# Fourier stage of a two-block network: its inputs loaded in the projection before it, the attention's queries loaded after its channel step

## The reference

```python
def fourier_mix(u, w_four):
    B, L, _ = u.shape
    ug = u.astype(jnp.float32).reshape(B, L, FOUR_GROUPS, FOUR_DIM)
    f = jnp.fft.fft2(ug, axes=(1, 3), norm="ortho").real
    return f.reshape(B, L, D_FOUR).astype(u.dtype) @ w_four

(fx, fgx, nqx, nkx, nvx, ngx, gqx, gkx, gvx, ggx, zfx, zbx) = jnp.split(hx @ w_in[l], IN_SPLITS, axis=-1)
na_x = neighbourhood_attention(split_heads(nqx, NA_HEADS), split_heads(nkx, NA_HEADS),
                               split_heads(nvx, NA_HEADS), nkc_h, nvc_h, rpb[l])
four_x = fourier_mix(fx, w_four[l])
mix_x = jnp.concatenate([four_x * jax.nn.silu(fgx), na_x * jax.nn.silu(ngx), gla_x * jax.nn.silu(ggx)], axis=-1)
x_new = x + gate_x[:, None, :] * (mix_x @ w_out[l])
```

## Time and profile before

| | us |
|---|---|
| median of the 3 runs | 4332.79 |
| lowest and highest run | 4326.86, 4337.24 |
| the profiled execution, span from its first to its last instruction | 4326.4 |
| PE busy in it | 3967.8 (92%) |
| DVE, ACT, POOL busy | 2036.2, 1432.6, 683.4 |
| Fourier block, first layer: first issue to the next block's first issue | 786.0 to 883.6 |
| Fourier block, second layer: first issue, and first POOL instruction of the next block | 2155.7, 2245.8 |

### The profile page before, as it was taken

How to read it: one execution, slowest core, us unless ns; L and a number is a source line. 1 busy time by engine, 2 the same in 40 slices (tenths; PEclk the granted TensorE clock), 3 DMA queues, 4 the chain that set the end, 5 groups by cost and what they waited for, 6 DMA issues and landing times. The chain is left out here.

```text
span 4326.4 us, 66533 instructions
## 1 busy us (share of the span) xinstructions
PE 3967.8 (92%) x25359; PEld 3241.8 (75%) x25359; DVE 2036.2 (47%) x4616; ACT 1432.6 (33%) x3255; POOL 683.4 (16%) x761
## 2 busy tenths in 40 slices
PE   6999999899679799999999869799999989979799
PEld 4777789777568688778977658677777867868687
DVE  5365111167656542111127567632750456657554
ACT  5000444256422310144327523321111467721211
POOL 3021000223120210000032220131430001000100
PEclk8999999999889899999999989899999989989899
DMA  5244221731256422222273345432111143357221
GB/s 195 90 147 143 82 77 61 230 136 59 100 196 220 175 100 73 95 76 77 75 240 106 113 146 198 173 112 90 64 71 66 47 134 102 103 214 255 79 77 64
DMA packets 215264, 525.90 MB, mean 122 GB/s; under 512 B 27478, under 2 KB 88392, under 8 KB 205604
## 3 DMA queue, kind: packets, MB, share of 16 engines
q1 hardware_dynamic: 188740, 438.91, 29.2%
q0 software_dynamic: 26208, 82.74, 5.4%
HBM read 330.43 MB, written 191.13 MB: 121 GB/s over the span
## 5 line engine op out<-in xcount | busy, mean ns | idle before, releaser
L72 PE MATMUL tm_tacc<-tm_tw_hi,hT_hi 128*128 128x384 f32 (+1 forms) x1120 | 414.6, 370 | 17.2 <-DVE tm_tw_lo L906 10.0
L73 PE MATMUL tm_tacc<-tm_tw_lo,hT_hi 128*128 128x384 f32 (+1 forms) x1120 | 410.0, 366 | 0.0
L74 PE MATMUL tm_tacc<-tm_tw_hi,hT_lo 128*128 128x384 f32 (+1 forms) x1120 | 410.0, 366 | 0.0
L72 PE MATMUL tz_tacc<-tz_tw_hi,hT_hi 128*128 128x512 f32 x896 | 359.4, 401 | 6.0 <-POOL tz_tw_lo L935 4.1
L72 PE MATMUL cm_acc<-hT_hi,cm_wb_hi 128*128 128x512 f32 (+1 forms) x912 | 362.2, 397 | 0.0
L73 PE MATMUL tz_tacc<-tz_tw_lo,hT_hi 128*128 128x512 f32 x896 | 355.0, 396 | 0.0
L74 PE MATMUL tz_tacc<-tz_tw_hi,hT_lo 128*128 128x512 f32 x896 | 355.0, 396 | 0.0
L74 PE MATMUL cm_acc<-hT_hi,cm_wb_lo 128*128 128x512 f32 (+1 forms) x912 | 344.3, 378 | 0.0
L73 PE MATMUL cm_acc<-hT_lo,cm_wb_hi 128*128 128x512 f32 (+1 forms) x912 | 343.9, 377 | 0.0
L788 DVE SCALAR_TENSOR_TENSOR tm_ds<-tm_dg,tm_ds 128x512 f32<-128x512 f32 (+1 forms) x40 | 25.6, 639 | 532.1 <-ACT tm_ds L782 532.1
L72 PEld LDWEIGHTS tm_tacc<-tm_tw_hi,hT_hi 128*128 128x128 f32 x1120 | 210.9, 188 | 59.1 <-DVE tm_tw_lo L906 13.6
(11 more groups left out here) (405 smaller groups left out, 8770.1 us busy)
## 6 DMA issues: line engine op xcount, KB each, us to landing
scr_z<-tz_tz SPq DMA_DIRECT2D x112, 256.0 KB
scr_zcm<-cm_zo SPq DMA_DIRECT2D x96, 256.0 KB, 2.0
scr_ztm<-tm_tz SPq DMA_DIRECT2D x68, 256.0 KB, 2.0
scr_xres<-out_x POOLq DMA_DIRECT2D x34, 512.0 KB, 4.1
cm_area<-in_w_ada POOLq DMA_DIRECT2D x64, 256.0 KB, 3.0
scr_z<-out_xn POOLq DMA_DIRECT2D x32, 512.0 KB, 4.8
mo_z<-scr_z SPq DMA_DIRECT2D x16, 1024.0 KB
tz_traw<-in_w_in SPq DMA_DIRECT2D x7, 2048.0 KB, 8.4
```

What stands on the lines that cost most here:

```text
L72: nc.tensor.matmul(out, ah, bh, start=start, stop=False)
L73: nc.tensor.matmul(out, ah, bl, start=False, stop=False)
L74: return nc.tensor.matmul(out, al, bh, start=False, stop=stop)
```

## The change

- `project_tm` gets `ahead`, a `FourierInputs`. In the last chunk, after the store of tile 3, SP waits until the last weights have been split (from then on `traw` is free) and issues `dch`, `wf` and image channels 0 to 127, `fx[0]` (1024 KB), into the place of `traw`. After the store of the last tile but one, SP waits for `decays.finished` and issues image channels 128 to 255, `fx[1]` (1024 KB), into the place of the decay buffers. The wait for the decay sums at the block's end goes.
- `fourier_phase` no longer issues `dch`, `wf` and `fx`. The context's channels come by themselves (`fc`, 256 KB, first layer only). PE waits for `f0_in` and `f1_in` in place of `fx_in`, and for `fc_in` ahead of the context's tiles.
- The queries' space is the one in which `dch`, `wf` and `fx[0]` lie, so SP issues the keys first, then waits for the 16th tile of the channel step (`ab_mm` at `N2`), then issues the queries, and only then goes on to the stores of `yo`.
- The buffers of the Fourier phase are moved by two gaps, so that `yo` and `fc` lie in the place of `fx[1]`.

```diff
@@ project_tm, SP
                     sp.dma_start(dst(c, t), zo[n % 3][:, 0:widths[c]]).then_inc(z_out[n % 3], 16)
+                    if ahead and c == n_chunks - 1 and t == 3:
+                        sp.wait_ge(lo_dve, KC // 2 * n_chunks)
+                        sp.wait_ge(lo_pool, KC // 2 * n_chunks)
+                        ahead.first(sp)
+                    if ahead and c == n_chunks - 1 and t == tiles[c] - 2:
+                        decays.finished(sp)
+                        ahead.second(sp)
             total = at[n_chunks]
             for j in range(3):
                 sp.wait_ge(z_out[j], 16 * ((total + 2 - j) // 3))
-            if decays:
+            if decays and not ahead:
                 decays.finished(sp)
@@ FourierInputs
+    def place(self, name):
+        at = lambda n, shape, offset: self.nc.alloc_sbuf_tensor_at(f"{name}_{n}", shape, F32, offset=offset)
+        self.dch, self.wf = at("dch", [128, 2, 2, 256], self.raw_at), at("wf", [128, 2, 256], self.raw_at + 4096)
+        self.fx = [at("fx0", [128, LX], self.raw_at + 6144), at("fx1", [128, LX], self.sums_at)]
+
+    def first(self, sp):
+        l, io = self.l, self.io
+        self.place(f"fa{l}")
+        sp.dma_start(self.dch[:, :, :, :], io["dft_ch"]).then_inc(self.w_in, 16)
+        sp.dma_start(self.wf[:, :, :], io["w_four"][l:l + 1, :, :, :].rearrange("a p k n -> p (a k) n")).then_inc(self.w_in, 16)
+        sp.dma_start(self.fx[0][:, :], io["zcm"][0, :, 0:LX]).then_inc(self.f0_in, 16)
+
+    def second(self, sp):
+        sp.dma_start(self.fx[1][:, :], self.io["zcm"][1, :, 0:LX]).then_inc(self.f1_in, 16)
@@ fourier_phase, SP
-                sp.dma_start(dch[:, :, :, :], io["dft_ch"]).then_inc(w_in, 16)
-                sp.dma_start(wf[:, :, :], io["w_four"][l:l + 1, :, :, :].rearrange("a p k n -> p (a k) n")).then_inc(w_in, 16)
-                sp.dma_start(fx[:, :, 0:LF], io["zcm"][0:2, :, 0:LF].rearrange("c p t -> p c t")).then_inc(fx_in, 16)
                 sp.dma_start(d1[:, :, :, :], io["dft_1"]).then_inc(d1_in, 16)
                 sp.dma_start(d2[:, :, :], io["dft_2"]).then_inc(d2_in, 16)
                 sp.dma_start(dc[:, :, :, :], io["dft_ctx"]).then_inc(d2_in, 16)
+                if first:
+                    sp.dma_start(fc[:, :, :], io["zcm"][0:2, :, LX:LT].rearrange("c p t -> p c t")).then_inc(fc_in, 16)
                 na.load_lines(sp, io)
-                na.load_tokens(sp, io)
+                na.load_keys(sp, io)
+                sp.wait_ge(ab_mm, N2)
+                na.load_queries(sp, io)
@@ fourier_phase, PE
-                pe.wait_ge(w_in, 32)
+                pe.wait_ge(fi.w_in, 32)
...
-                pe.wait_ge(fx_in, 16)
+                pe.wait_ge(fi.f0_in, 16)
+                pe.wait_ge(fi.f1_in, 16)
```

More of the change, by code:

```diff
@@ L709, in __init__ @@
     def __init__(self, P, src, width):
+        self.at = P.nc.sbuf_base
         self.raw = P.sb("traw", [128, KC, 512])
@@ L723, in __init__ @@
         self.nc, self.l, self.io = nc, l, io
+        self.sb_at = nc.sbuf_base
         self.z, self.wa, self.ba = P.sb("dz", [128, 512]), P.sb("dwa", [128, 128]), P.sb("dba", [128, 4])
@@ L796, in finished, with project_tm @@
         sp.wait_ge(self.b_out, 16 * 20)
-def project_tm(P, nc, hT, first, w, dst, widths, funcs, tiles, heads=None, spatial=None, decays=None, turn=None):
+def project_tm(P, nc, hT, first, w, dst, widths, funcs, tiles, heads=None, spatial=None, decays=None, turn=None, ahead=None):
     n_chunks, width = len(funcs), max(widths)
@@ L1048, in load_lines, with load_queries, load_keys @@
             eng.dma_start(self.lines[:, 1, x, :], bass.AP(cols.tensor, cols.offset, [[0, QR], [GRID, QC], [1, GRID]])).then_inc(self.lines_in, 16)
-    def load_tokens(self, eng, io):
+    def load_queries(self, eng, io):
         eng.dma_start(self.q[:, :, :], io["zcm"][2:5, :, 0:LX if self.last else LT].rearrange("c p t -> p c t")).then_inc(self.q_in, 16)
+    def load_keys(self, eng, io):
         eng.dma_start(self.kk[:, :, :], io["zcm"][5:8, :, :].rearrange("c p t -> p c t")).then_inc(self.k_in, 16)
@@ L1102, in bias, with __init__, under, fourier_phase @@
         self.build(dve, 0)
-def fourier_phase(nc, l, io, keep, na):
+class FourierInputs:
+    def __init__(self, nc, l, io, last):
+        self.nc, self.l, self.io = nc, l, io
+        self.LF = LX if last else LT
+        self.w_in, self.f0_in, self.f1_in = [nc.alloc_semaphore(f"fa{l}_{n}") for n in ("w_in", "f0_in", "f1_in")]
+    def under(self, raw_at, sums_at):
+        self.raw_at, self.sums_at = raw_at, sums_at
+    def place(self, name):
[10 more added lines that the diff above has]
+        sp.dma_start(self.fx[1][:, :], self.io["zcm"][1, :, 0:LX]).then_inc(self.f1_in, 16)
+def fourier_phase(nc, l, io, keep, na, fi):
     with phase(nc, f"four{l}") as P:
-        dch = P.sb("dch", [128, 2, 2, 256])
-        wf = P.sb("wf", [128, 2, 256])
+        dch, wf, fx = fi.dch, fi.wf, fi.fx
         w2 = P.sb("w2", [128, 2, 512])
-        fx = P.sb("fx", [128, 2, LT])
         d1 = P.sb("d1", [128, N2, 3, 128])
@@ L1118, in fourier_phase @@
         NAB = N2 if na.last else N2 + 2
-        LF = LX if na.last else LT
         ab = P.sb("ab", [128, N2 + 2, 512])
+        P.sb("gap0", [128, (fi.sums_at - nc.sbuf_base) // 4])
         yo = [P.sb(f"yo{j}", [128, 512]) for j in range(4)]
+        fc = P.sb("fc", [128, 2, LC])
+        P.sb("gap1", [128, (fi.sums_at + 10848 - nc.sbuf_base) // 4])
         fo = P.sb("fo", [128, NX, 256])
         acc = [P.ps(f"acc{b}") for b in range(6)]
-        fx_in, w_in, d1_in, d2_in, w2_mm, w2_ok, ab_mm, ab_dve, ab_act, y_mm, y_ev, o_mm, o_ev = [P.sem(s) for s in (
-            "fx_in", "w_in", "d1_in", "d2_in", "w2_mm", "w2_ok", "ab_mm", "ab_dve", "ab_act", "y_mm", "y_ev",
+        fc_in, d1_in, d2_in, w2_mm, w2_ok, ab_mm, ab_dve, ab_act, y_mm, y_ev, o_mm, o_ev = [P.sem(s) for s in (
+            "fc_in", "d1_in", "d2_in", "w2_mm", "w2_ok", "ab_mm", "ab_dve", "ab_act", "y_mm", "y_ev",
             "o_mm", "o_ev")]
@@ L1199, in channels @@
                     for k in range(2):
[L1200 removed]
+                        lhs = fx[k][:, t:LX:N2] if t < N2 else fc[:, k, (t - N2) * 128:(t - N2 + 1) * 128]
                         last = nc.tensor.matmul(acc[2 + t % 2][:, :], lhs, w2[:, k, :], start=(k == 0), stop=(k == 1))
@@ L1228, in _ @@
                 if first:
+                    pe.wait_ge(fc_in, 16)
                     for t in range(N2, NAB):
@@ L3169, in first_layer @@
     xin = (lambda g: io["x"] if g < 4 else io["ctx"]) if l == 0 else (lambda g: io["z2"][0:LX, D:2 * D] if g < 4 else io["z2"][0:LC, 2 * D:3 * D])
+    fi = FourierInputs(nc, l, io, last)
     with phase(nc, f"tw{l}") as W:
@@ L3188, in first_layer @@
                 tiles = [NX if last else NT] * 2 + [NT] * 2
+                decays = DecaySums(P, nc, l, io, tiles)
+                fi.under(first.at, decays.sb_at)
                 project_tm(P, nc, hT, first, lambda c: io["w_gate" if c < 2 else "w_val"][l * 2 + c % 2, :, :, :],
                            lambda c, t: io["ztm"][t * 128:(t + 1) * 128, (c * 512 if c < 2 else 256 + c * 384):(c * 512 + 512 if c < 2 else 640 + c * 384)],
-                           [512, 512, 384, 384], [ACT.Silu] * 2 + [ACT.Copy] * 2, tiles, decays=DecaySums(P, nc, l, io, tiles))
+                           [512, 512, 384, 384], [ACT.Silu] * 2 + [ACT.Copy] * 2, tiles, decays=decays, ahead=fi)
     with phase(nc, f"pre{l}") as Q:
@@ L3195, in first_layer @@
             na = Neighbourhood(P, last)
-            fourier_phase(nc, l, io, keep, na)
+            fourier_phase(nc, l, io, keep, na, fi)
             pre.place(P, LX if last else LT)
```

## The result

The changed kernel takes 4341.14 us (median of 13 runs, 4336.87 to 4346.68) against 4329.87 us before (13 runs): a ratio of 1.0025 [1.0017, 1.0033]. That is 11.3 us slower where I forecast 0.5 us less, and above the range that I gave (4323 to 4340 us). The profiled execution has a span of 4339.3 us, 12.9 us more than the earlier trace rows.

The account below looks back on a forecast made before the run. PE takes nearly all of the span, so loads matter only where PE waits. Gains of 7.9 us less 7.4 us for a later block start gave -0.5 us, 4332.3 us on the median; range 4323 to 4340 us.

Parts of the forecast that it names:

- T0 does not stay: Projection's end: fx[1] delays the last store, so T0, SP's first issue in the Fourier block, moves 3.69 us per layer.
- Rival 2: Projection's end: fx[1] does not hold the last store; T0 moves 0.5 us per layer; 4325.9 us; chance 0.12.
- Loads gone from the head of the block: Fourier block's head: PE starts at T0, channel step ends at T0 + 34.65 and 35.93 us; 10.0 us of waiting removed.
- What I had put at nothing in the projection: Projection's last chunk: three loads behind tile 3 and the wait for the decay sums cost nothing.
- The queries behind the channel step: First transform: queries ahead of yo stores take 12.5 and 11.4 us, leaving 7.9 of the 10.0 us gained.
- rival 3: First transform: queries need their old 18.3 and 17.7 us and become the new stall; +11.6 us, 4344.4 us; chance 0.09.
- Rival 1: First transform: queries do not hold the yo stores and PE is not stopped; -5.6 us, 4327.2 us; chance 0.13.

Follow-up runs that it names:

- the run without gathers: Changed kernel with POOL's 48 gathers moved behind its wait for the queries, so the two no longer run together: 4356.23 us, one run.
- the query step alone: Kernel before with only the load order changed: keys first, queries after the channel step's 16th tile, then the yo stores: 4345.44 us, ratio 1.0029.

## Why the prediction was wrong

**"T0 does not stay" held.** It gave 3.69 us per layer by `fx[1]`'s 5.3 us and 0.53 us for the store behind it; measured are 3.75 and 3.63 us, with `fx[1]` at 5.4 and 5.2 us. The store's semaphore came 0.5 us behind the load ahead of it, and with the load behind the store the shift was gone. Rival 2 is out. I had weighed a rule there, from "DMA: Bandwidth & Descriptors", section "Queues, rings and completion order" in the Trainium skill: of its two halves, the second agrees with the landing. But the trace does not test it, since the store's own rows moved only behind those of the load (787 to 788.6 us): the data were late already, before any wait of the semaphore.

**"Loads gone from the head of the block" held** but for PE's speed: PE started 0.05 us after T0, and its first matmuls took 6.55 and 6.12 us where I took 5.46 and 6.71 us; the channel step ended at T0 + 35.82 and T0 + 35.38 us, 0.6 us in sum off. What I had put at nothing in the projection was nothing: ACT and PE waited for no DMA in its last chunk, in either layer.

**"The queries behind the channel step" is the step that failed**, in the size of its main term: "I take 12.5 us" and "I take 11.4 us" measured 16.0 and 14.7 us. I had chosen between 10.6 us (9.7 in the second layer), by a stretch at 405 GB/s, and 13.6 us (12.3), by one with gathers at 302 GB/s. Both are the price of nearly all of the load, but not of its end. Below are the packets of SP's queue (count, MB, share of the engines), first with the change from 826.5 to 839.6 us. Then come, for the run without gathers, the issue of the queries, the packets from 827.4 to 838 us, and all packets from 838 to 841.2 us. A row of the queries is a packet of 9 KB, a row of a `yo` store one of 2 KB.

```profile
q1 hardware_dynamic: 382, 3.51, 85.3%
...
827.43 0.37 SPq L1060 DMA_DIRECT2D nain_q<-scr_zcm  x1
q1 hardware_dynamic: 369, 3.40, 89.8%
DMA packets 562, 1.11 MB, mean 348 GB/s; under 512 B 71, under 2 KB 71, under 8 KB 547
```

So with the change 3.51 of the 3.54 MB had started 13.1 us after the issue, near the price with gathers, and without gathers 3.40 MB had started 10.6 us after it, the price without them. But the load landed 16.0 and 13.7 us after its issue: the last few rows took another 2.9 and 3.1 us, while rows of the `yo` stores behind them moved already (without gathers 547 of 562 packets, the other 15 being the end of the queries). In the second layer it is the same: 11.8 and 9.7 us, then 2.9 and 2.8 us for the end. Of the 3.5 and 3.3 us by which I was short, 0.6 and 0.4 us lie in the part beside which the gathers ran (13.1 and 11.8 us where I took 12.5 and 11.4 us). The other 2.9 us in each layer are this end, which is in neither price, though both hold the 1.9 us of a small store. Why the last rows come so late is open. The fit in the same page of the Trainium skill, section "Anatomy of one DMA", had given an estimate of 10.1 and 9.2 us; no run here agrees with it for a load that starts beside others: 12.5 to 19.1 us in all versions that load in one piece.

With 16.0 and 14.7 us, PE's restart came at T0 + 53.57 and T0 + 52.16 us instead of T0 + 49.62 and T0 + 49.55 us: a gain of 1.4 us instead of 7.9 us. That is 6.5 us of the error.

**A cost that I left out** is PE's clock after the longer stall, 1.65 + 1.73 = 3.4 us. The stall of 1.71 us in the kernel before left the granted clock at 1.00, so no row near it warned. But the forecast itself holds a stall of 3.2 us in the first layer (T0 + 49.62 less T0 + 46.39), nearly twice the old one, and rival 3 a longer one; there the clock should have been priced. In the run without gathers a stall of 3.48 us was already followed by a granted 0.50:

```profile
842.61 0.79 PE L1263 MATMUL four_acc<-four_ab,four_d 128*128 128x128 f32 x2 [3.48 <-ACT four_yo L1325]
843.00:846.00 3.00, 3.00 (x16) 3.00 (x16) 0.00 (x0) 0.21 (x1) 3.00 (x7) 0.50 0.83 218
```

Together the two terms are 9.9 us; the sum of -0.5 us becomes +9.4 us, against 11.3 us measured, with an interval of 7.4 to 14.3 us.

**The rivals.** The result, +11.3 us, is nearly the +11.6 us of rival 3, which named the mechanism, but by luck in its size: the queries took 16.0 and 14.7 us and not the 18.3 and 17.7 us that it priced, and the clock's 3.4 us, which it lacked too, made up for most of that. For the same reason it decided earlier than at its 17.1 and 16.0 us. Its sign, queries that land 16 us or more after the channel step, was there in the first layer alone. Rival 1 is out: ACT did wait. The keys, which I said would land earlier, did (21.4 against 32.0 us), and it was worth nothing, since nothing waited for them any longer.

**Left open.** Why the last rows of the queries take about 3 us, and why the same load takes from 16.0 to 19.1 us (first layer) in versions that issue it at about the same point. The gathers issued around it land later in the longer cases (median 8.2 us in the change, 9.1 us in the kernel with the query step alone, 10.6 us with `fx[1]` behind the last store), but what delays them was not separated. A version that loads the queries early, into a space of their own, was not tried.

## What to carry to other kernels

A load put ahead of stores in one queue costs what it lasts less the slack of the buffers behind it, and its price is that of the nearest row with the same neighbours, not of the best rate seen, and with some us for its last rows (about 3 us here). Where a large load must pass such a queue, cut it into pieces that fit between the stores, or give it another queue; and ask of every early load which last store or semaphore stands behind it, since the stage ends there. When a wait may grow to several us on TensorE, price the clock after it as well.

## What the runs showed of the hardware that I had not expected

- Small gathers take much of the engines' time for few bytes: 48 of 32 KB each, with no load beside them, hold the 16 engines at a share of 0.68 and move 96 GB/s; beside the end of the keys they took 64.4% of the time for 0.26 MB. The keys issued 6 us ahead of them landed after 21.4 us, without them after 14.5 us.
- A second queue does not free a transfer from another's: with the queries on ACT's queue, ACT still waited 4.44 us for the first `yo` store.
- A load lands with its last rows: 3.51 of the 3.54 MB of the queries had started 13.1 us after the issue, but the load landed after 16.0 us.
- Twelve pieces of 288 KB landed in 4.3 us (the median; the last three in 6.9 to 7.2 us, first layer) beside the stores, and cost no stall in the first transform.
- Stalls of 6.02 and 5.04 us cost another 1.65 and 1.73 us by PE's clock; one of 1.71 us cost none, with 1.00 granted behind it.
